# A two-layer decoder trunk on one core: the last projection tile cut into column halves, the first scaled piece read by two engines, three pieces transposed ahead

## The reference

```python
for i in range(DEPTH):                       # DEPTH = 2
    mod = cond @ ada_w[i] + ada_b[i]
    sh_m, sc_m, g_m, sh_f, sc_f, g_f = split(mod, 6)
    hm = _rms(x, norm_mix[i]) * (1.0 + sc_m) + sh_m
    y = _nsa_mixer(hm, ...) if i == 0 else _mla_mixer(hm, ...)   # ends with  o @ w_out
    x = x + g_m * y
    hf = _rms(x, norm_ffn[i]) * (1.0 + sc_f) + sh_f
    a, b = split(hf @ w_in, 2)
    x = x + g_f * ((silu(a) * b) @ w_out)
```

## Time and profile before

| | |
|---|---|
| median of three runs | 737.58 us (736.84 to 737.87) |
| profiled execution, its own time | 737.94 us |
| its span (first to last instruction) | 736.1 us |
| PE busy | 699.7 us, 95% of the span |
| DVE, ACT, POOL busy | 525.1, 373.4, 98.2 us |
| PE's three instructions of a product, with their 568 + 176 repetitions each | 226.6 + 218.6 + 218.9 and 70.1 + 68.5 + 69.0 us |
| PE waiting for the low part of tokens, all transposes | 8.1 us in 6 waits |

### The profile page before, as it was taken

The page is one execution under the profiler, slowest core; times in us unless marked ns, Lnnn a source line. Parts: engine busy times, 40 slices in busy tenths (PEclk is TensorE's granted clock), DMA queues, the critical chain, the costliest instruction groups (busy, mean ns, idle before and its releaser), DMA issues. The chain is left out here.

```text
span 736.1 us, 10780 instructions
## 1 busy us (share of the span) xinstructions
PE 699.7 (95%) x3903; PEld 575.5 (78%) x3903; DVE 525.1 (71%) x981; ACT 373.4 (51%) x696; POOL 98.2 (13%) x182
## 2 busy tenths in 40 slices
PE   3699999999989999999999999889999999999997
PEld 1577768888878888878878897778888888878886
DVE  3346687898888889887786578977767755554444
ACT  3244566577447444444333379676465444444341
POOL 7020212022110111221111100600001000000000
PEclk9999999999999999999999999999999999999999
DMA  8997996032248999997798372601538766554521
GB/s 289 351 371 187 372 369 228 2 116 86 90 170 262 334 326 354 321 342 273 265 341 289 94 211 66 228 1 59 172 111 276 230 189 193 171 173 171 204 83 57
DMA packets 93742, 155.09 MB, mean 211 GB/s; under 512 B 5979, under 2 KB 68064, under 8 KB 93696
## 3 DMA queue, kind: packets, MB, share of 16 engines
q1 hardware_dynamic: 80768, 111.24, 46.0%
q0 software_dynamic: 12928, 43.24, 17.3%
HBM read 151.32 MB, written 1.05 MB: 207 GB/s over the span
## 5 line engine op out<-in xcount | busy, mean ns | idle before, releaser
L776 ACT ACTIVATE w_hi<-raw 128x1024 fp32r<-128x1024 f32 (+3 forms) x198 | 201.5, 1024 | 263.2 <-PE lin L1810 238.3
L1121 DVE TENSOR_TENSOR w_lo<-raw,w_hi 128x1024 fp32r<-128x1024 f32 (+3 forms) x198 | 233.2, 1185 | 119.3 <-ACT w_hi L776 118.8
L1808 PE MATMUL lin<-w_hi,st_hi 128*128 128x512 f32 (+2 forms) x568 | 226.6, 399 | 2.3 <-DVE w_lo L1121 2.0
L1810 PE MATMUL lin<-w_hi,st_lo 128*128 128x512 f32 (+2 forms) x568 | 218.9, 385 | 0.0
L1809 PE MATMUL lin<-w_lo,st_hi 128*128 128x512 f32 (+2 forms) x568 | 218.6, 385 | 0.0
L1808 PEld LDWEIGHTS lin<-w_hi,st_hi 128*128 128x128 f32 x568 | 107.3, 189 | 28.1 <-issue 6.1
L1810 PEld LDWEIGHTS lin<-w_hi,st_lo 128*128 128x128 f32 x568 | 107.3, 189 | 21.3
L1809 PEld LDWEIGHTS lin<-w_lo,st_hi 128*128 128x128 f32 x568 | 107.6, 189 | 19.3 <-issue 0.7
L613 POOL DMA_DIRECT2D ada_ring<-in_ada_w_dram x80 | 42.7, 534 | 324.8 <-DVE acc L1205 238.7
L1205 DVE SCALAR_TENSOR_TENSOR acc<-ada_ring,cond_b,acc 128x1024 f32<-128x1024 f32 x64 | 81.8, 1279 | 3.3 <-DMA ada_ring<-in_ada_w_dram 3.1
L1808 PE MATMUL lin<-w_hi,hid_hi 128*128 128x512 f32 x176 | 70.1, 398 | 0.0
(11 more groups left out here) (257 smaller groups left out, 858.1 us busy)
## 6 DMA issues: line engine op xcount, KB each, us to landing
raw<-in_ffn_w_in_dram SPq DMA_DIRECT2D x88, 512.0 KB, 5.2
ada_ring<-in_ada_w_dram POOLq DMA_DIRECT2D x80, 512.0 KB, 6.3
raw<-in_ffn_w_out_dram SPq DMA_DIRECT2D x22, 1024.0 KB, 6.1
raw<-in_nsa_w_in_dram SPq DMA_DIRECT2D x10, 1024.0 KB, 12.6
ada_first<-in_ada_w_dram SPq DMA_DIRECT2D x8, 1024.0 KB, 13.1
raw<-in_nsa_cmp_w_dram SPq DMA_DIRECT2D x4, 1024.0 KB, 9.9
raw<-in_nsa_w_out_dram SPq DMA_DIRECT2D x4, 1024.0 KB, 8.6
raw<-in_mla_w_out_dram SPq DMA_DIRECT2D x4, 1024.0 KB, 5.1
```

Source lines behind the costliest of these rows:

```text
L776: nc.scalar.activation(part_of(w_hi, s), raw_part(s), ACT.Copy).then_inc(hi_ready, 1)
L1121: nc.vector.tensor_tensor(part_of(w_lo, s), raw_part(s), part_of(w_hi, s).bitcast(F32), ALU.subtract).then_inc(lo_ready, 1)
L1808: nc.tensor.matmul(bank, a_h, w_h, start=first, stop=False)
L1810: return nc.tensor.matmul(bank, a_l, w_h, start=False, stop=last)
```

## The change

It edits the norms' surroundings in seven ways.

1. `last_unit`: tile 1's 512 columns become two parts of 256, `left` in its `lin` bank and `right` in the `tp` bank that is free. All parts do slots 0 and 1, then tile 0, then left, then right do slots 2 and 3.
2. `update_x` follows: three multiplications and additions, of 512, 256 and 256 columns, in place of two of 512. The squares are regrouped: tile 0's 1024 columns in one instruction, tile 1 in pieces of 512, 256 and 256.
3. The first piece (k = 0) is transposed twice, into both `tp` banks. ACT writes `st_hi` straight from one (`modulated`), DVE scales the other into `tfull` and subtracts (`direct_low`).
4. Columns 512 to 1023 are normalised after the first piece's low part (`normalise_half(1)`).
5. `norm_start` transposes three pieces ahead and drops its second group of idle matmuls; a `tp` bank counts as empty as soon as the scaling has read it, not when the low part is done.
6. At norm 1 the gate row is copied by ACT; DVE makes two low parts of weights before the last `ada_sum`, and one more before the update. At norm 2 the low part of the first weight slot moves between the two tiles of the update, and ACT's high parts are spread among the squares.
7. At the start of the kernel `first_pair` transposes ahead of its wait for the tokens' low part.

```diff
+TAIL = 256
+RESID = (5, 4, 5, 4)
+RESID_BEFORE = (0, 5, 9, 14)
+SQUARES = 2, 4, 3, 4
...
+                added = RESID_BEFORE[k - 1] + RESID[k - 1]
                 if not column_halves:
                     high_to(s + 2)
-                squares_of_x(k, 0)
-                squares_of_x(k, 1, [0])
-                high_to(s + 2)
-                squares_of_x(k, 1, [1])
+                    if k == 1:
+                        act.wait_ge(ada_red, ada_at(2))
+                        nc.scalar.activation(gate_rows[:, 0, 0:512], sc[0][:], ACT.Copy)
+                        nc.scalar.activation(gate_rows[:, 0, 512:D], sc[1][:], ACT.Copy).then_inc(ada_out, 1)
+                    square_of_x(1, 1, 0, D // 2, added - 3)
+                    square_of_x(0, 0, 0, D, added - 2)
+                    square_of_x(2, 1, D // 2, D - TAIL, added - 1)
+                    square_of_x(3, 1, D - TAIL, D, added)
...
                 for m, (k0, nk) in enumerate(PIECES):
-                    scaled_high(batch0 + m, k0, nk, scale_cols[:, norm, k0:k0 + nk],
-                                ada_cols[:, shift_seg, k0:k0 + nk])
+                    if m == 0:
+                        scaled_count[0] += 1
+                        act.wait_ge(tp_filled, batch0 + 1)
+                        nc.scalar.activation(st_hi[:, k0, :], tp[batch0 % 2][:, 0:S], ACT.Identity,
+                                             scale=scale_cols[:, norm, k0:k0 + 1],
+                                             bias=ada_cols[:, shift_seg, k0:k0 + 1]).then_inc(st_high, 1)
+                    else:
+                        scaled_high(batch0 + m + 1, k0, nk, scale_cols[:, norm, k0:k0 + nk],
+                                    ada_cols[:, shift_seg, k0:k0 + nk])
...
+            def direct_low(norm, shift_seg, batch, k0):
...
+                dve.wait_ge(tp_filled, batch + 1)
+                nc.vector.tensor_scalar(full, tp[batch % 2][:, 0:S], scale_cols[:, norm, k0:k0 + 1],
+                                        ada_cols[:, shift_seg, k0:k0 + 1], ALU.mult, ALU.add).then_inc(tokens_read, 1)
+                dve.wait_ge(tokens_read, count_before(TP_EMPTIED, batch + 1, "read"))
+                dve.wait_ge(st_high, counts["st"])
+                nc.vector.tensor_tensor(st_lo[:, k0, :], full, st_hi[:, k0, :].bitcast(F32),
+                                        ALU.subtract).then_inc(st_ready, 1)
...
-            for last, n in ((5, 2), (6, 2), (7, 1), (8, 0)):
+            for last, n in ((5, 2), (6, 2), (8, 1)):
                 low_to(OUT0 + last)
+                if n == 1:
+                    modulation(1, 4)
                 ada_sum(n)
-            modulation(1, 4)
-            low_to(OUT0 + 9)
-            ada_row(2, 0)
+            low_to(OUT0 + 10)
             dve.wait_ge(ada_out, ada_at(2))
...
-                for tiles, slots in ((range(T), (0, 1)), ((0,), (2, 3)), ((1,), (2, 3))):
+                pe.wait_ge(*emptied(next_batch - 2))
+                whole = (lin[2 * (unit % 2)], 0, 0, 512)
+                left = (lin[2 * (unit % 2) + 1], 1, 0, TAIL)
+                right = (tp[next_batch % 2], 1, TAIL, 512)
+                for parts, slots in (((whole, left, right), (0, 1)), ((whole,), (2, 3)), ((left,), (2, 3)),
+                                     ((right,), (2, 3))):
...
                 idle_into(sc[1], n)
-                for m in range(2):
+                for m in range(3):
                     x_batch(batch0, m)
-                idle_into(sc[1], IDLE_SECOND)
...
-                pe.wait_ge(st_ready, stationary_number(T_H0) + q + 1)
                 if q + 2 < BLOCKS:
                     x_batch(T_H0, q + 2)
+                stationary_done(T_H0 + q)
```

More of the change, by code:

```diff
@@ L112 @@
 FIRST_PIECES = ((0, 2), (2, 2), (4, 2), (6, 2))
+TOKEN_RELEASE = ("high", "read", "scaled", "scaled", "scaled", "scaled")
 def _batches(n, *who):
@@ L117, in _batches @@
     return len(TP_EMPTIED) - n
-T_H0 = _batches(len(FIRST_PIECES), "st")
+T_H0 = _batches(len(FIRST_PIECES), "scaled")
 T_KVC = _batches(2, "act")
@@ L133 @@
 T_O0 = _batches(len(PIECES), "st")
-T_HF0 = _batches(len(PIECES), "st")
+T_HF0 = _batches(len(PIECES) + 1, *TOKEN_RELEASE)
 T_HID0 = _batches(FU, "st")
-T_H1 = _batches(len(PIECES), "st")
+T_H1 = _batches(len(PIECES) + 1, *TOKEN_RELEASE)
 LATENTS = ((3, 2), (0, 2), (2, 1))
-T_CQ = _batches(len(LATENTS), "st")
+T_CQ = _batches(len(LATENTS), "scaled")
 T_K1 = _batches(6, "act")
@@ L184, in stationary_number @@
 def stationary_number(batch):
-    return count_before(TP_EMPTIED, batch, "st")
+    return sum(o in ("st", "scaled", "high") for o in TP_EMPTIED[:batch])
 VEC_GAIN, VEC_LAT, VEC_PE, VEC_NSA, VEC_QK = 0, 32, 37, 69, 73
@@ L1853, in last_unit @@
                             row_done()
-                    if tiles == (0,):
+                    if right not in parts:
                         ins.then_inc(part_done, 1)
```

206 lines of the change are left out of this document (120 added, 86 removed).

## The result

| | before | after |
|---|---|---|
| median, same chip | 736.38 us (20 executions) | 732.80 us (20 executions) |
| profiled execution, its own time | 737.94 us | 733.38 us |
| its span | 736.1 us | 731.6 us |

A forecast was written before the change was run, and what follows sets the result against it. PE is busy 95%, so time is won only where it does no product, chiefly at norms. Terms 1.07 + 1.5 + 0.1 + 0.3 = 3.0 us off 737.94, less 0.36 for the median, give 734.6 us; range 732.7 to 736.4.

The forecast's parts named there:

- The chain: At norm 3, one unbroken, exposed chain from PE's last product to the next unit's first product, 8.16 us without a product.
- the overlap behind the transposes: From the first transposes to block 2 at each norm: forecast to save 0.48 us at norm 3, 0.7 at norm 1.
- a stall of 0.14: At norm 3, piece 1's low part seen at 3.6 while block 0's products end at 3.46, so PE waits 0.14 us.
- block 2 starts at 5.80: At norms 3 and 1, block 2 comes 5.80 us after the first transposes, in place of 6.28 and 6.50.
- ScalarE sees no third-piece delay: At norm 2, ScalarE has the same work and its three pieces in a row set the limit; 0.1 us saved.
- the tail at norm 3: Column split of the last tile: update 0.54 us and square 0.25 saved, split costs 0.2; transposes 0.59 us earlier net.
- the update at norm 1: Updates start at 207.6 in place of 208.39 and the root chain at 213.8, not 214.58: 0.8 us earlier.
- ScalarE's copies: At norm 1, ScalarE copies the gate in two operations of at most 0.63 us each, done near 207.6.
- The start: Transposes ahead of the wait for the low part at the kernel's start gain 0.3 us, between 0 and 0.4, up to 1.5.
- The filler wasn't missed: Rival: without the second idle group the clock falls behind norms; 736.3 with one fall, 739.7 with three. Chance 0.08.
- Only the tail counts: Rival: early pieces take longer behind the transposes, so the 0.48 and 0.7 us savings vanish; 735.8 us. Chance 0.17.
- More than drawn: Rival: start clock recovers sooner, DVE's read of `tp` and the gate copies cost less; 732.8 us. Chance 0.10.

The follow-up runs named there:

- e1: The changed kernel with the start's edit undone (next piece's transposes behind the wait for the low part again): 734.34 us, ratio to before 0.9972.
- e3: The changed kernel with tile 1 of the last projection unit whole again (512 columns, one bank): 733.28 us, ratio to before 0.9955.
- e4: The changed kernel with the first piece transposed once and scaled by ScalarE alone, at all norms: 733.23 us, ratio to before 0.9949.
- e5: The changed kernel with the order around the gate at norm 1 as before, gate copies on DVE: 734.13 us, ratio to before 0.9963.
- e7: The changed kernel with the second token half normalised straight behind the first, ahead of the first piece's low part: 733.41 us, ratio to before 0.9959.
- e8: The changed kernel with two pieces transposed ahead, five more idle matmuls, third piece behind the first's low part: 735.86 us, ratio to before 0.9983.
- e9: The changed kernel with two pieces transposed ahead, without the second group of idle matmuls: 734.61 us, ratio to before 0.9964.
- e10: The changed kernel with nine extra matmuls, 2.1 us of PE, behind norm 0's products: 735.19 us, ratio to before 0.9969.
- e11: The changed kernel with the first piece in one bank at norm 2 only, scaled by ScalarE alone there: 733.11 us, ratio to before 0.9945.
- e12: The changed kernel itself, unaltered, profiled and measured again on another chip: 732.85 us, ratio to before 0.9946.
- e2: The kernel before with the start's edit alone (banks released by the scaling, transposes ahead of the wait): 736.38 us, ratio to before 0.9997.

## Where the prediction failed, and what of it held

**The time.** 732.8 lies 1.8 us under my 734.6, outside the forecast's own range (733.5 to 735.7) and only 0.1 inside the wide one (732.7 to 736.4). Of the 1.8, 1.2 us is the base: I took the kernel before at the median of three executions, 737.58, and twenty gave 736.38. The spread between executions was larger than several terms of my sum, and the range did not carry it. The other 0.6 us is a gain of 3.6 where I had summed 3.0; in the trace the three norms alone gave 3.53 where I had 2.67.

**The step that failed.** The chain held, and so did the places where time is won. Wrong was the overlap behind the transposes, at all three norms: "a stall of 0.14", "block 2 starts at 5.80", and at norm 2 "ScalarE sees no third-piece delay". I let the later pieces hold PE up. With 512 columns the runs show no such wait: once the first product has started, block 2 follows 3.63 to 3.66 us later at norms 1 and 3 in the change and in e1, e3, e4, e5, e7, e8, e9, e10, e11 and e12. The overlap gave 0.78, 1.01 and 0.42 us where I had 0.48, 0.7 and 0.1: 0.9 us too little in all. That was partly made up by the tail at norm 3, which I had 0.22 too high. The second size that was wrong is the update at norm 1, 0.3 too low.

**Norm 3, forecast 1.07, measured 1.11.** The number is right by luck, as two errors cancel. The tail was to give 0.59 and gave 0.37: the split costs 0.30 and not 0.2 (half products stand 0.120 apart, not the 0.118 of the earlier trace rows, and whole ones 0.227, not 0.23), and the root chain starts 1.66 behind PE's end, 0.75 earlier, of which 0.06 is lost in the chain's first operation (0.22; with two numbers to add in place of three it took 0.16). I had put it at nothing. The idle matmuls end just where the transposes are due, and cost nothing that the rows show. The overlap was to give 0.48 and gave 0.78 (0.37 and 0.78 make 1.15; the last 0.04 is below what these rows tell).

The term behind it is a handover. I had PE see ScalarE's high part 0.26 us late (1.08 to 1.34), as it saw DVE's low part before, and so put the second piece's transposes at 1.34 and the first product at 2.0. The rows after have the high part ended at 538.45 and those transposes at 538.50, 0.05 later: they come at 1.16, the first product at 1.84 in place of 2.0, and the second piece's low part, ended at 3.10 and not 3.34, is there before PE asks for it at 3.30, so the stall of 0.14 goes. That makes the 0.30. DVE's read of `tp` took 0.54 and not 0.45. Its low part ended 0.15 ahead of the first product; in e4, where PE visibly waits for the low part, the same step takes 0.14. So the first product may have waited for DVE as much as for PE's own six transposes; the rows don't part the two.

**Norm 1, forecast 1.5, measured 1.98.** The update was to start 0.8 earlier, and did so by 1.08 (2.09 between the rows, less the 1.01 from ahead). The reduction was 0.17 late against the first attention, where I had 0.24, and the modulation cost 0.17 + 0.17, my 0.35. Mis-sized were ScalarE's copies: each takes 0.6, but the second starts 0.50 behind the first, so both end 1.13 behind the reduction, not 1.26; the rest is the reduction itself, 0.07 earlier and 0.06 shorter than I put it. From the update to the root chain it took 6.23, as forecast (6.20). The overlap gave 1.01 for the 0.7, by the same step as at norm 3; 0.07 was lost in the root chain. The Trainium skill, SBUF — State Buffer, Who interferes with whom, says that a tensor_scalar in a two-port mode and GpSimd exclude each other. The operation that took 0.77 beside a memset takes 0.17 away from it, and 0.76 in e5, where it stands beside one again (203.11, the memset at 202.87 for 0.97), which agrees.

**Norm 2, forecast 0.1, measured 0.44.** The step that failed is "ScalarE sees no third-piece delay". It did, in the kernel before, and the row was there to read:

```profile
426.31 1.02 ACT L813 ACTIVATE tfull<-tp,ada_cols,scale_cols 128x256 f32<-128x256 f32 x2 [0.48 <-DVE st_lo L1172]
```

ScalarE scaled the third piece 2.92 behind the transposes at 423.39, after 0.48 of idling, as PE turned that piece only behind the first low part. With the change it does so at 2.55. I had read that the same work must take the same time, and missed the wait in it.

**The start, forecast 0.3.** At one clock level 0.2 to 0.4 was seen at 60 us, from one profile without the edit at each level, and e10 shows that time there passes to the end. By medians it is between 0.1 and 1.5, so the term is not confirmed. The full clock at the start, my upper end of 1.5, does occur, but with and without the edit.

**The rivals.** The filler wasn't missed: the granted clock is 1.00 in all three holes after. Only the tail counts: false, the overlap gave more than the tail. More than drawn, 732.8, is the number that came, but by luck: 1.2 us of the way to it is the base, the clock at the start was not the edit's doing, DVE's read cost more than I took, and only the copies cost less (0.13). Chunks from memory took nothing back in the profile after, and 0.4 us in e12. Of the signs that I had named, the time to the first product at norm 3 (6.7, measured 6.67), the one at norm 1 (7.1, measured 6.96) and the clock came as said; half products stood 0.120 apart, not 0.118; norm 2 was shorter at block 2 too, and not only at its first product; the copy of the gate ended at 206.27, with the 1.01 from ahead 207.28 on the old scale, not 207.6.

## What to carry to other kernels

When a unit starts on tokens that arrive in pieces, find out first whether PE runs without a gap from the first product on. If it does, only the first product's time counts, and what stands ahead of it on PE (filler, a later piece's transposes) costs whatever of it sticks out behind the wait that it fills: the same ten idle instructions were hidden before and cost 0.55 us in e8. If products are too narrow for that, the engine that prepares the pieces counts, and giving the first piece a second bank costs the second piece its own. The parts of such a change don't add up: undone one by one (e3, e4, e5, e8) they cost 0.5, 0.4, 1.2 and 2.75 us, together 4.8, where the whole brings 3.5.

To compare kernels whose executions differ by more than the edit brings, use short stretches of the trace between two rows that both kernels have. The holes agreed to 0.04 us where medians scattered by 0.5. Long stretches are no better than medians: from 142 us to the end the same kernel took 590.0 and 590.5. And take the base of a forecast from many executions: three of them were 1.2 us off.

## What the runs showed of the hardware

The same instructions ran at a granted clock of 0.68 or of 1.00 near 20 and near 35 us, by the execution: the change and e8 are the same up to norm 1, and differ so. The fall near 35 us goes with 1.6 us at 60 us. In e2 the clock fell once more, behind a wait of 2.21 us for a chunk:

```profile
101.11:105.00 3.89, 3.89 (x18) 2.78 (x19) 3.51 (x13) 2.05 (x2) 0.53 (x1) 0.69 1.03 399
```

After, with a wait of 1.85 there, it stayed at 1.00 over the 3.9 us behind it, and in e8 with one of 2.20 too. What decides it remains open.
